# A two-block transformer kernel on one core: fp32r scores on stacked halves, values taken tile by tile, and the second gate vector on TensorE

## The reference, cut to what matters

```python
mod = silu(c) @ w_ada + b_ada                 # six blocks of 1024; gt2 is the last
sh1, sc1, gt1, sh2, sc2, gt2 = split(mod, 6)
q, k, v, bg, cg, hv = split(modulate(rmsnorm(x), sh1, sc1) @ w_in)
q, k = apply_rope(q), apply_rope(k)           # 8 query heads, 2 key heads, 64 wide
# each block of 128 queries sees [sink, 256 context keys, its own and the neighbouring
# blocks of keys with |i-j| <= 128]: 512 keys (blocks 0 and 3) or 640 (blocks 1 and 2)
p = softmax(concat([sink, q @ k_ctx.T * scale, where(valid, q @ k.T * scale, -inf)]))
att = p_ctx @ v_ctx + p_loc @ v_loc
x = x + gt1 * (concat([att, conv]) @ w_out)
x = x + gt2 * expert_choice_ffn(modulate(rmsnorm(x), sh2, sc2))
```

## Time and profile before

| | us |
|---|---|
| median of 3 runs | 2501.95 (2501.6 to 2503.89) |
| the profiled execution's own time | 2502.74 |
| its span | 2501.0 |
| PE busy in the span | 2458.6 (98%) |
| DVE / ACT / POOL busy | 1132.8 / 735.2 / 49.5 |
| mean granted TensorE clock | 0.994 of full speed |

### The profile page before, as it was taken

How to read it: one execution, slowest core, us unless ns; L and a number is a source line. 1 busy time by engine, 2 the same in 40 slices (tenths; PEclk the granted TensorE clock), 3 DMA queues, 4 the chain that set the end, 5 groups by cost and what they waited for, 6 DMA issues and landing times.

```text
span 2501.0 us, 29717 instructions
## 1 busy us (share of the span) xinstructions
PE 2458.6 (98%) x11265; PEld 1802.0 (72%) x11265; DVE 1132.8 (45%) x1732; ACT 735.2 (29%) x1049; POOL 49.5 (2%) x28
## 2 busy tenths in 40 slices
PE   7999999999999999999999999999999999999999
PEld 4876744434437888888888888888887667888887
DVE  6785312222227444336444334444337565544422
ACT  4245210100014333224333223333224354333321
POOL 0042000000000000000000000000000000000000
PEclk8999999999999999999999999999999999999999
DMA  7552699999992223313222322323222211223332
GB/s 309 191 168 98 262 408 421 421 420 421 421 407 89 98 94 112 102 55 110 92 100 99 104 91 84 101 92 113 96 90 68 80 43 43 93 92 101 105 104 68
DMA packets 84654, 404.29 MB, mean 162 GB/s; under 512 B 9176, under 2 KB 9560, under 8 KB 60896
## 3 DMA queue, kind: packets, MB, share of 16 engines
q1 hardware_dynamic: 84576, 403.22, 43.3%
HBM read 401.08 MB, written 2.10 MB: 161 GB/s over the span
## 4 chain that ended last, share of the span: by engine, by line
PE 92%; DVE 4%; ACT 2%; DMA 1%; issue 1%; SPq 0%; ACTq 0%; DVEq 0%
PE pair L1142 23%; PE pair L1144 23%; PE pair L1143 23%; PE pair L1438 9%; PE pair L1463 4%; PE pair L1374 2%; PE pair L1693 1%; PE pair L1831 1%; PE pair L1402 1%; PE pair L1288 1%; PE pair L1801 1%; PE pair L1802 1%; DMA ada_first<-in_w_ada 1%; PE pair L1403 1%; DMA stage<-in_gate 0%
## 5 line engine op out<-in xcount | busy, mean ns | idle before, releaser
L1856 DVE TENSOR_TENSOR wL<-stage,wH 128x1024 fp32r<-128x1024 f32 (+3 forms) x301 | 389.0, 1292 | 775.0 <-ACT wH L699 774.5
L1142 PE MATMUL pair<-hH,wH 128*128 128x512 f32 x1672 | 658.4, 394 | 8.5 <-DVE hL L1966 2.9
L1144 PE MATMUL pair<-hH,wL 128*128 128x512 f32 x1672 | 651.7, 390 | 0.0
L1143 PE MATMUL pair<-hL,wH 128*128 128x512 f32 x1672 | 651.6, 390 | 0.0
L699 ACT ACTIVATE wH<-stage 128x1024 fp32r<-128x1024 f32 (+3 forms) x301 | 335.2, 1114 | 842.1 <-PE pair L1144 842.1
L1142 PEld LDWEIGHTS pair<-hH,wH 128*128 128x128 f32 x1672 | 314.4, 188 | 80.3 <-DVE hL L1901 4.2
L1143 PEld LDWEIGHTS pair<-hL,wH 128*128 128x128 f32 x1672 | 314.5, 188 | 66.9 <-issue 2.4
L1144 PEld LDWEIGHTS pair<-hH,wL 128*128 128x128 f32 x1672 | 314.4, 188 | 65.8
L1142 PE MATMUL pair<-gH,wH 128*128 128x512 f32 x704 | 273.9, 389 | 0.0
L1143 PE MATMUL pair<-gL,wH 128*128 128x512 f32 x704 | 273.9, 389 | 0.0
L1144 PE MATMUL pair<-gH,wL 128*128 128x512 f32 x704 | 273.9, 389 | 0.0
(11 more groups left out here) (365 smaller groups left out, 2135.1 us busy)
## 6 DMA issues: line engine op xcount, KB each, us to landing
ring<-in_experts SPq DMA_DIRECT2D x182, 1024.0 KB, 19.5
stage<-in_gate SPq DMA_DIRECT2D x88, 512.0 KB, 3.2
stage<-in_up SPq DMA_DIRECT2D x88, 512.0 KB, 3.2
stage<-in_down SPq DMA_DIRECT2D x64, 704.0 KB, 4.0
adaw<-in_w_ada SPq DMA_DIRECT2D x32, 512.0 KB, 5.2
stage<-in_w_in SPq DMA_DIRECT2D x18, 512.0 KB, 3.7
ring<-in_experts SPq DMA_DIRECT2D x16, 512.0 KB, 11.4
stage<-in_mla_in SPq DMA_DIRECT2D x9, 512.0 KB, 3.3
```

The source lines that it names most:

```text
L1142: pe.matmul(ps, lh, rh, start=first, stop=False)
L1143: pe.matmul(ps, lh, rl, start=False, stop=False)
L1144: return pe.matmul(ps, ll, rh, start=False, stop=last)
L1856: dve.tensor_tensor(low, stage[:, n % STAGE, 0:w], high, ALU.subtract).then_inc(strip_lo, 1)
```

## The change

1. **Scores in fp32r on stacked halves.** After the rope, ACT makes an fp32r high part of each q and of K (`high_part`) and DVE the low part (`low_half`), both in tiles shared by all r (`part_q`, `part_k`). SP then copies them by DMA from SBUF to SBUF (`stacked`: four DMAs of 64x512 for a q, eight of 64x768 for K) so that the 64 high rows and the 64 low rows of one head lie on the 128 partitions of `qS`, and K's high (or low) part twice in `kS`. A score is then two fp32r matmuls over 128 rows for each piece of at most 512 columns. `kZ` and its zeroing on POOL go. Since `part_q` is reused, ACT's `high_part(r)` waits until the DMAs of the r before have landed (`qk_moved`).
2. **Values tile by tile.** PE iteration u takes one key tile of the block before (two 64-column products) instead of all at once; `PT` has two places.
3. **The last modulation block on TensorE.** Eight w_ada tiles are loaded in SP's steps 6 to 13; PE multiplies each at the end of steps 9 to 16 (`gate_part`: four f32 matmuls with 32 weight columns and 256 moving ones, each in its own 32 columns of the array), and turns the row at the end (`gate_turn`). POOL's work and PE's L1349 go.
4. **The convolution's high and low parts** move into units 6, 8, 10 and 12, the last modulation takes behind the first unit's mask.
5. The staging tiles of the first 26 strips are cut to 1024 columns to free room; masks come as one table after V is turned.

```diff
+        GATE_LOAD, GATE_AT = 6, 9
+        CONV_AT = (6, 8, 10, 12)
+        MASK_AT = (5 * P, 0, C, 0)
+        MOVES = 16 * (4 * 4 + 8)
...
+        kv_tiles = {0: [4, 5, 0, 1], 1: [4, 5, 0, 1, 2], 2: [1, 2, 3, 4, 5], 3: [4, 5, 2, 3]}
+
+        def key_pieces(n):
+
+            return {0: [(0, 0, 512)], 1: [(128, 0, 384), (512, 384, 256)], 2: [(128, 384, 384), (512, 0, 256)],
+                    3: [(0, 0, 256), (256, 512, 256)]}[n]
...
+            def stacked(r):
+
+                sp.wait_ge(qk_lo, r + 1)
+                for part in range(2):
+                    if r == K_AT:
+                        for j in range(2):
+                            for at in range(0, P, 64):
+                                sp.dma_start(kS[at:at + 64, j, part, :].bitcast(F32), part_k[64 * j:64 * j + 64, part, :].bitcast(F32)).then_inc(qk_moved, 16)
+                    else:
+                        for j in range(2):
+                            at = 64 * (j ^ part)
+                            sp.dma_start(qS[j][at:at + 64, ROT_Q[r], :].bitcast(F32), part_q[64 * j:64 * j + 64, part, :].bitcast(F32)).then_inc(qk_moved, 16)
+
             def gate_tile(j):
 
-                if j == 0:
+                if j < 4:
                     sp.wait_ge(strip_used, V_AT + 1)
                 else:
-                    sp.wait_ge(ada_added, max(24, 2 * j + 21))
-                sp.dma_start(gate_w[j % 2][:, :], A["w_ada"][j * P:j * P + P, 5 * 1024:6 * 1024]).then_inc(gate_landed[j % 2], 16)
+                    sp.wait_ge(gate_used, j - 3)
+                sp.dma_start(gate_w[j % 4][:, :], A["w_ada"][j * P:j * P + P, 5 * 1024:6 * 1024]).then_inc(first_or_gate_landed[j % 4], 16)
...
+                if GATE_LOAD <= s < GATE_LOAD + KD:
+                    gate_tile(s - GATE_LOAD)
+                if s - 2 in ROT_AT:
+                    stacked(ROT_AT[s - 2])
+                if s == 12:
+                    sp.wait_ge(v_turned, 2)
+                    sp.dma_start(window[:, :], A["window"]).then_inc(window_loaded, 16)
...
-                    pool.tensor_scalar(gate_acc[:, :], gate_w[0][:, :], stat[:, 0:1], None, ALU.mult).then_inc(ada_added, 1)
...
-                    pool.tensor_scalar(w[:, :], w[:, :], stat[:, j:j + 1], None, ALU.mult).then_inc(ada_added, 1)
...
-                    pool.tensor_tensor(gate_acc[:, :], gate_acc[:, :], w[:, :], ALU.add).then_inc(ada_added, 1)
...
+            def high_part(r):
+
+                act.wait_ge(rope_done, r + 1)
+                if r == K_AT:
+                    act.wait_ge(strip_used, V_AT + 1)
+                    ins = act.activation(part_k[:, 0, :], kT[:, :], ACT.Copy)
+                else:
+                    if r:
+                        act.wait_ge(qk_moved, 64 * r if r < K_AT else 64 * (r + 1))
+                    ins = act.activation(part_q[:, 0, :], qT[:, ROT_Q[r], :], ACT.Copy)
+                ins.then_inc(qk_hi, 1)
...
                 hi(s + 2)
                 copy_out(s)
+                if s - 1 in ROT_AT:
+                    high_part(ROT_AT[s - 1])
+                if s == 17:
+                    act.wait_ge(gate_used, KD)
+                    act.activation(gate_row[:, :], pb[6][:, 0:256], ACT.Copy).then_inc(gate_rowed, 1)
...
-                if n and a == j == 0:
-                    act.wait_ge(pv_done, n)
+                if n >= 2 and a == j == 0:
+                    act.wait_ge(pv_done, n - 1)
...
+            def gate_part(j):
+
+                pe.wait_ge(first_or_gate_landed[j % 4], 32 + 16 * (j // 4 + 1))
+                if j == 0:
+                    pe.wait_ge(std_done, NCTX + 1)
+                for g in range(4):
+                    mm = pe.matmul(pb[6][32 * g:32 * g + 32, 0:256], stat[:, j:j + 1].broadcast_to([P, 32]), gate_w[j % 4][:, 256 * g:256 * g + 256],
+                                   start=(j == 0), stop=(j == KD - 1))
+                mm.then_inc(gate_used, 1)
+
+            def gate_turn():
+
+                pe.wait_ge(gate_rowed, 1)
+                for i in range(2):
+                    mm = pe.transpose(pb[6][:, 256 + i * P:256 + (i + 1) * P], gate_row[:, i * P:(i + 1) * P], tab("ident"))
+                mm.then_inc(mod_summed, 1)
...
+                if GATE_AT <= s < GATE_AT + KD:
+                    gate_part(s - GATE_AT)
                 if s in SUM_AT:
                     mod_sum(SUM_AT[s])
+                if s == 17:
+                    gate_turn()
...
-                q = qT[:, a, n * P:(n + 1) * P]
-                pe.matmul(pb[2 * j][:, 0:C], q, kZ[:, j, T:T + C], start=True, stop=True)
-                mm = pe.matmul(pb[2 * j][:, C:2 * C], q, kZ[:, j, lo_:lo_ + C], start=True, stop=True)
-                if hi_ - lo_ > C:
-                    mm = pe.matmul(pb[2 * j + 1][:, 0:hi_ - lo_ - C], q, kZ[:, j, lo_ + C:hi_], start=True, stop=True)
+                q = qS[j][:, a, n * P:(n + 1) * P]
+                for at, key, w in key_pieces(n):
+                    pe.matmul(pair[j][:, at:at + w], q, kS[:, j, 0, key:key + w], start=True, stop=False)
+                    mm = pe.matmul(pair[j][:, at:at + w], q, kS[:, j, 1, key:key + w], start=False, stop=True)
                 mm.then_inc(scored, 1)
...
+            def att_values(n, k):
+                if k == 0:
+                    pe.wait_ge(pt_act, 8 * n + 8)
+                    pe.wait_ge(v_ready, 2)
+                    if n == 0:
+                        pe.wait_ge(mod_ready, 6)
+                    else:
+                        pe.wait_ge(att_lo, n)
                 tiles = len(kv_tiles[n])
...
+                v = kv_tiles[n][k]
+                for j in range(2):
+                    mm = pe.matmul(pb[7][64 * j:64 * j + 64, :], V[:, v, 64 * j:64 * j + 64], PT[n % 2][j][:, k, :],
+                                   start=(k == 0), stop=(k == tiles - 1))
+                if k == tiles - 1:
+                    mm.then_inc(pv_done, 1)
...
-                if block_at(u - LAG1 - 1) is not None:
-                    att_values(block_at(u - LAG1 - 1))
+                n, k = divmod(u - LAG1 - 1 - 7, 8)
+                if 0 <= n < NB and k < len(kv_tiles[n]):
+                    att_values(n, k)
...
-            for m in range(KD):
-                mm = pe.matmul(pb[3][:, m:m + 1], gate_acc[:, m * P:(m + 1) * P], ones[:, 0:1], start=True, stop=True)
-            mm.then_inc(mod_summed, 1)
...
+            def low_half(r):
+
+                dve.wait_ge(qk_hi, r + 1)
+                if r == K_AT:
+                    ins = dve.tensor_tensor(part_k[:, 1, :], kT[:, :], part_k[:, 0, :], ALU.subtract)
                 else:
-                    dve.tensor_tensor(dst, dst, tmp, ALU.add).then_inc(rope_done, 1)
+                    ins = dve.tensor_tensor(part_q[:, 1, :], qT[:, ROT_Q[r], :], part_q[:, 0, :], ALU.subtract)
+                ins.then_inc(qk_lo, 1)
...
+                if s - 2 in ROT_AT:
+                    low_half(ROT_AT[s - 2])
...
+                if u == 0:
+                    last_blocks()
+                if u in CONV_AT:
+                    conv_low(CONV_AT.index(u))
+                if block_at(u - LAG1 - 6) is not None:
+                    att_low(block_at(u - LAG1 - 6))
```

198 lines of the change are left out of this document (91 added, 107 removed).

## The result

The changed kernel takes **2529.6 us** (median of 4 runs, 2528.89 to 2531.18) against 2502.81 of the kernel before (2501.6 to 2503.89): a ratio of 1.0108, 95% interval 1.0091 to 1.0126. It is slower by 27 us; the forecast was 11 us slower, 2513, with a range up to 2526. So the direction was right, and the size lies outside the range.

A forecast was written before the change was run, and what follows sets the result against it. PE was taken to bound the in-projection, with PE, DVE and ACT taking turns in the attention. Stalls 11.4, gate parts 5.3, turns 0.25, L1349 -0.5 and attention -5.2 summed to +11.2 us: 2513 us, range 2504 to 2526.

The forecast's parts named there:

- The stalls: In-projection: PE waits 3.5, 2.0, 2.2 and 3.7 us behind the moves of q and K, 11.4 us in all.
- K's term: In-projection, step 7: K's eight moves, issued in 3 us and landed at 115.0, make PE wait 3.7 us.
- The upper bound: In-projection: with 4.6 us per landing, the slowest strip's time, the stalls reach 18.6 us.
- Gate parts: In-projection: four-group matmuls of 0.45 us plus 0.30 us array change, 0.75 a part; seven count, 5.3 us.
- The eighth part: In-projection: one of the eight gate parts lies in the stall of step 9 and is not counted.
- Attention: First attention, first scores to first out-projection: 75.0 us against 80.2, a gain of 5.2 us.
- L1349: Router: removing PE's 3.55 us of work, which stood in a wait for DVE's softmax, gives back 0.5 us.
- Rival "the moves are hidden": In-projection: DMAs land before ACT has the rope, stalls are 0, attention gains 10 us: 2497 us; chance 0.09.
- Rival "column groups do not run together": Gate parts on PE cost 2.0 us each instead of 0.75, adding 9 us: 2522 us; chance 0.12.
- Rival "clock falls": In-projection: PE's clock drops in the new stalls, adding 3 to 8 us: 2519 us; chance 0.12.
- Rival "scores no faster": Attention: weight loads bind the short score matmuls, so the 5 us gain goes: 2518 us; chance 0.05.
- The signs: Expected in the profile: late strip high part, PE idling before steps 7 to 10, gate-part times, attention 72 to 78 us, later stages shifted.

The follow-up runs named there:

- e4: The changed kernel with SP issuing the moves ahead of the w_ada loads in each step, instead of behind them: 2518.5 us.
- e1: The changed kernel with two places in turn for q's high and low parts instead of one: 2509.0 us.
- e10: As e5, but the eight gate parts stand in two rows of four, after steps 12 and 16: 2509.5 us.
- e5: The changed kernel with two places for q's parts and the moves issued ahead of the w_ada loads: 2506.4 us.
- e9: As e5, but the last modulation block as in the kernel before, on POOL during the attention and summed by PE after the router's logits: 2508.5 us.
- e11: As e9, but the convolution's high and low parts made before the first unit, as in the kernel before: 2503.6 us.
- e12: The changed kernel with only the convolution's high and low parts put back before the first unit: 2528.0 us.
- e13: As e5, with the convolution's high and low parts made before the first unit: 2505.0 us.
- e3: The changed kernel with 60 and 74 useless matmuls filling PE's two long waits, before the rotation of step 6 and before step 10: 2528.3 us.
- e3b: As e3, mended: 66 fillers ahead of PE's wait for ACT's copy of q, and 88 before step 10: 2529.3 us.
- e2: As e1, but only one of the eight gate parts is loaded and multiplied: 2506.6 us.
- e8: The changed kernel with the moves issued by POOL on a queue of its own, instead of by SP behind the loads: 2525.5 us.

## Why the prediction was right and wrong

- **The stalls (11.4 us, bounds 0 to 18.6): mechanism right, size wrong. This is the step that failed.** PE idled 20.2 us (7.92, 1.76, 0.18 and 10.30), in place of 3.5, 2.0, 2.2 and 3.7. The step as put: "A move is 128 KB behind 1 MB of other loads: I take 2.2 us, near the small one". It named the megabyte ahead and then took the row of an empty queue. Measured: landings of 5.80, 4.02 and 6.76 us and an issue of 0.60 us a move, not 0.4 (its own row gives 0.48: three issues in 1.44). In the order of e4 the moves land in 2.3 us and PE waits 10.8 us, near the 11.4 in part by luck (see e4): the path from the high part to the rope holds, K's term doesn't. The upper bound failed too: the slowest strip (4.6) was no bound for a move behind several loads, and the eight moves of K, 1.5 MB, were given the landing of a single one.
- **That the place is what binds:** shown by e1, 20.6 us from a second place.
- **Gate parts (5.3 us):** a single one measures 0.76 us, predicted 0.75; groups together and the change at 0.30 to 0.33 both hold (e10). The eighth part was taken as free in a stall. In e5 it costs little too: PE waits 0.75 for the tile, works 0.76 and waits 0.41 where e9, without the part, waits 2.85. But "loads are early enough" failed: gate tiles were waited for (0.6 to 1.5 us in the kernels with two places), and with them in the queue DVE's w_ada tile landed at 116.7 to 119.1 us, against 115.4 and 116.2 in e9 and e11.
- **Attention (-5.2, 75.0 us):** 75.6. An iteration with values took 2.34 us (predicted 2.28), and a handing over of the convolution's parts 1.0 to 1.1 us of idling and 0.69 of work, as said. That the whole is within 0.6 us rests on a sum of many stretches, whose single terms were not measured. Part 4 is worth some 1.5 us (e12, e13).
- **L1349 (-0.5):** the rest of the kernel is 0.85 us shorter, of which PE's new wait in the router's softmax, 2.74 us where 3.55 of work stood, explains 0.8.
- **Rival "the moves are hidden" (0.09):** wrong; ACT's strip high part stood at 91.17.
- **Rival "column groups do not run together" (0.12):** wrong.
- **Rival "clock falls" (0.12):** it fell, to 0.50, but filling the waits gave 0.3 to 1.3 us instead of 3 to 8 (e3, e3b), less than the runs can tell. Time at a lower clock inside a stretch that another loop bounds is not to be added to that loop's waits.
- **Rival "scores no faster" (0.05):** wrong.
- **The signs:** four held (strip high part after 86 with a DMA's end ahead of it, gate parts of 0.43 with 0.33 around them, attention in 72 to 78, the rest shifted as a whole: 2264.3 to 2267.7 us in all profiles). "2 to 4 us before steps 7, 8, 9 and 10" did not.

The books of the change without its stalls (e5, +3.4 us of span): scores +8.3 (gate parts 6.0, their turn 0.25, small waits 1.2, and a remainder of 0.9, in which PE ran at a clock of 0.58 for 4 us after a gate part and V's turns), attention -4.65, rest -0.25. The forecast's sum without stalls was -0.15. What it lacked is the eighth part, the small waits, the remainder and 0.6 us in the attention. These are PE's books. They do not say what taking the gate off PE would give back: e9 does, 4.0 us of the 8.3; what stays, 4.2, is mostly the 2.85 us that PE waits there before step 10, behind the moves, and the lower clock after it (0.71 and 0.87 in 120 to 128 us).

Left open: what exactly the gate parts cost at the end (e2 gives 2.4 to 5.3 us for seven), and so how e13's last 2 us divide. Open too is what it would give to put the w_ada tile that DVE waits for ahead of K's moves.

## What to carry to other kernels

Price a DMA by what stands ahead of it in the queue and beside it on the engines, not by its size: the same 128 KB took 2.3 us ahead of the loads and 5.7 behind them, and a queue of their own brought them to 5.0. What stands behind the moves waits in turn: in the kernels with two places DVE idled 4 to 9.5 us for a w_ada tile issued after K's. A wait for a landing belongs where nothing else is behind it: here it stood ahead of the next strip's high part, and one more place of 4 KB a partition removed 20 us. Before calling a lower clock a loss, look which engine bounds that stretch: ahead of another engine's wait it cost nothing that could be told (e3), with nothing behind it to wait for some 2.5 us (e10).

## What the runs showed of the hardware

- Moves between SBUF places of 64 partitions, 192 KB each: eight of K land in 2.5 to 3.9 us with no load issued just ahead (e4) and 5.8 to 6.8 behind two loads. Issuing one costs SP 0.60 us (0.47 to 1.09), POOL 0.52 (e8); a load of 512 KB costs SP mostly 0.33 to 0.43.
- While K's moves ran, with loads beside them (changed kernel, 120 to 124 us), the engines were full (share 1.05 to 1.07) at 254 to 263 GB/s counted, where loads alone show 1.03 at 410 (148 to 156 us).
- Four column groups of 32 run as one: eight records in 0.43 us beyond the change.
- DVE's subtraction with two inputs: 0.69 us, and 1.76 beside POOL's work (e5, e9).
